# Turning the hidden chunks of five dense feed-forwards by a transposing DMA in place of TensorE

## What is computed

```python
def swiglu(h, w_gate, w_up, w_down):
    return (jax.nn.silu(h @ w_gate) * (h @ w_up)) @ w_down

x = x + swiglu(rmsnorm(x, norm), w_gate, w_up, w_down)      # second stack: 0.5 * swiglu
```

## Time and profile before

| | |
|---|---|
| time, median of 3 runs | 2066.12 us (2066.04 to 2066.29) |
| span of the profiled execution, first to last instruction | 2064.4 us |
| mean granted TensorE clock | 0.999 |
| busy: PE, DVE, ACT, POOL | 99%, 68%, 58%, 5% |
| DMA: moved, mean rate | 467.19 MB, 226 GB/s |

### The profile page before, as it was taken

The page is one execution under the profiler, slowest core; times in us unless marked ns, Lnnn a source line. Parts: engine busy times, 40 slices in busy tenths (PEclk is TensorE's granted clock), DMA queues, the critical chain, the costliest instruction groups (busy, mean ns, idle before and its releaser), DMA issues.

```text
span 2064.4 us, 27729 instructions
## 1 busy us (share of the span) xinstructions
PE 2036.4 (99%) x10169; PEld 1711.7 (83%) x10169; DVE 1411.3 (68%) x1558; ACT 1199.0 (58%) x1386; POOL 94.8 (5%) x140
## 2 busy tenths in 40 slices
PE   9999999999999999999999999999999999999999
PEld 9988888778888888887888877888888899888887
DVE  6655557688898898999554675455555579795454
ACT  4454458677777877776444565444544465875442
POOL 1010001000000000010100010000000000230000
PEclk9999999999999999999999999999999999999999
DMA  8555434389999998998555444555555455445551
GB/s 306 183 187 192 176 133 144 126 308 371 364 378 374 365 380 348 381 392 331 204 183 185 179 146 151 196 183 184 183 184 186 148 179 196 163 154 190 194 186 41
DMA packets 68273, 467.19 MB, mean 226 GB/s; under 512 B 7777, under 2 KB 8177, under 8 KB 13521
## 3 DMA queue, kind: packets, MB, share of 16 engines
q1 hardware_dynamic: 63616, 455.24, 59.5%
q10 hardware_dynamic: 3536, 8.10, 1.2%
q0 software_dynamic: 1024, 2.56, 0.5%
HBM read 461.11 MB, written 4.75 MB: 226 GB/s over the span
## 4 chain that ended last, share of the span: by engine, by line
PE 89%; DVE 5%; ACT 3%; issue 1%; DVEq 1%; ACTq 0%; POOL 0%; POOLq 0%
PE gu L2177 15%; PE gu L2179 15%; PE gu L2178 15%; PE acc L2177 10%; PE acc L2179 10%; PE acc L2178 10%; DVE wlo L1315 2%; PE acc L2273 2%; PE acc L2275 2%; PE acc L2274 2%; PE tp L2287 1%; ACT whi L715 1%; PE tp L2206 1%; PE acc L2732 1%; PE tp L2764 1%
## 5 line engine op out<-in xcount | busy, mean ns | idle before, releaser
L1315 DVE TENSOR_TENSOR wlo<-raw,whi 128x2048 fp32r<-128x2048 f32 (+2 forms) x422 | 956.4, 2270 | 351.1 <-ACT whi L715 350.4
L715 ACT ACTIVATE whi<-raw 128x2048 fp32r<-128x2048 f32 (+1 forms) x436 | 827.3, 1899 | 213.6 <-PE acc L2179 165.1
L2177 PE MATMUL gu<-whi,actA_hi 128*128 128x512 f32 x1408 | 560.0, 398 | 0.9 <-DVE wlo L1315 0.6
L2179 PE MATMUL gu<-whi,actA_lo 128*128 128x512 f32 x1408 | 549.3, 390 | 0.0
L2178 PE MATMUL gu<-wlo,actA_hi 128*128 128x512 f32 x1408 | 548.5, 390 | 0.0
L2179 PEld LDWEIGHTS gu<-whi,actA_lo 128*128 128x128 f32 x1408 | 264.7, 188 | 55.8
L2177 PEld LDWEIGHTS gu<-whi,actA_hi 128*128 128x128 f32 x1408 | 265.1, 188 | 54.5 <-issue 2.3
L2178 PEld LDWEIGHTS gu<-wlo,actA_hi 128*128 128x128 f32 x1408 | 265.4, 189 | 50.6
L2177 PE MATMUL acc<-whi,hT_hi 128*128 128x512 f32 x656 | 256.5, 391 | 0.5 <-DVE wlo L1315 0.5
L2179 PE MATMUL acc<-whi,hT_lo 128*128 128x512 f32 x656 | 255.9, 390 | 0.0
L2178 PE MATMUL acc<-wlo,hT_hi 128*128 128x512 f32 x656 | 255.7, 390 | 0.0
(11 more groups left out here) (452 smaller groups left out, 2351.5 us busy)
## 6 DMA issues: line engine op xcount, KB each, us to landing
raw<-in_slabs SPq DMA_DIRECT2D x427, 1024.0 KB, 4.9
y_rows<-big ACTq DMA_DIRECT2D x7, 512.0 KB, 5.1
raw<-in_slabs SPq DMA_DIRECT2D x4, 576.0 KB, 3.8
hT_hi<-cum_rows ACTq DMA_DIRECT2D x8, 256.0 KB, 3.9
hT_lo<-cum_rows ACTq DMA_DIRECT2D x8, 256.0 KB, 4.0
raw<-in_slabs SPq DMA_DIRECT2D x2, 768.0 KB, 4.2
raw<-in_slabs SPq DMA_DIRECT2D x2, 640.0 KB, 3.9
x<-in_x SPq DMA_DIRECT2D x2, 512.0 KB, 4.3
```

The source lines that it names most:

```text
L715: act.activation(whi[:, n0 % SPLIT, 0:w], raw[:, n0 % RAW, 0:w], ACT.Copy).then_inc(slab_hi, 1)
L1315: dve.tensor_tensor(wlo[:, n0 % SPLIT, 0:w], raw[:, n0 % RAW, 0:w], whi[:, n0 % SPLIT, 0:w].bitcast(F32), ALU.subtract).then_inc(slab_spli ...
L2177: pe.matmul(o, xh, wh, start=start, stop=False)
L2179: return pe.matmul(o, xl, wh, start=False, stop=stop)
```

## The change

In the dense feed-forwards, chunks 0 to 9 are no longer turned by PE. After the second silu, ACT waits for h_tok and copies it, seen as 16-bit integers, to two planes: the low halves of all 512 floats of a partition, then the high halves (`turned`). It waits for its own copy and issues one transposing DMA of 128x1024 16-bit elements into `h_turned`, as eight blocks of 128. At the next up_a position DVE copies the eight blocks back into floats with the halves side by side (`joined`, 1024 elements a partition), ACT makes hT_hi from that (`joined_hi`), and DVE makes hT_lo (`joined_lo`). PE's down product waits on hidden_lo. The order of the 128-column blocks in hT differs, which `hidden_cols` makes up for. Chunk 10 and the experts are turned by PE as before; a dense feed-forward counts one use of `tp` instead of 11.

```diff
@@ ffn_stage
-            stage("ffn", slabs=3 * C * experts, tp=C * experts, hi=C * experts, ...
+            turns = 1 if gates is None else C * experts
+            stage("ffn", slabs=3 * C * experts, tp=turns, hi=turns, ...
@@ views
+        h_planes = area(2560, 512).bitcast(U16).rearrange("p (w n) -> p w n", w=2)
+        h_turned = area(3072, 512).bitcast(U16).rearrange("p (b n) -> p b n", n=P)
+        hT_all = area(3584, 512)
+        hidden_halves = h_tok[:, :, :].rearrange("p t n -> p (t n)").bitcast(U16).rearrange("p (n w) -> p w n", w=2)
+        joined_halves = hT_all[:, :].bitcast(U16).rearrange("p (n w) -> p w n", w=2)
+        turned_halves = h_turned[:, :, :].rearrange("p (w b) n -> p w (b n)", w=2)
@@ ACT
+                def turned(c, i):
+                    act.wait_ge(gu_read, 2 * (f.c0 + c + 1) + 4 * i)
+                    act.activation(h_planes[:, :, :], hidden_halves, ACT.Copy).then_inc(hidden_planes, 1)
+                    act.wait_ge(hidden_planes, m0 + c + 1 + 2 * i)
+                    act.sem_inc(hidden_sent, 1)
+                    act.dma_start_transpose(h_turned[:, :, :], h_planes[:, :, :].rearrange("p w n -> p (w n)")
+                                            ).then_inc(hidden_turned, 16)
+                def joined_hi(c, i):
+                    act.wait_ge(hidden_joined, m0 + c + 1 + 2 * i)
+                    act.activation(hT[0], hT_all[:, :], ACT.Copy).then_inc(hidden_hi, 1)
...
+                        if dense and k != 3 * C - 3:
+                            turned(c, i)
+                    elif kind == "up_a" and k and dense:
+                        joined_hi(c - 1, i)
@@ DVE
+                def joined(c, i):
+                    dve.wait_ge(hidden_turned, 16 * (m0 + c + 1) + 32 * i)
+                    dve.tensor_copy(joined_halves, turned_halves).then_inc(hidden_joined, 1)
+                def joined_lo(c, i):
+                    dve.wait_ge(hidden_hi, m0 + c + 1 + 2 * i)
+                    dve.tensor_tensor(hT[1], hT_all[:, :], hT[0].bitcast(F32), ALU.subtract).then_inc(hidden_lo, 1)
...
-                        if k:
+                        if k and dense:
+                            joined(c - 1, i)
+                            joined_lo(c - 1, i)
+                        elif k:
                             t_lo(c - 1, i, ex)
@@ PE
-                        pe.wait_ge(tp_read, f.u0 + c + 1 + 2 * i + C * ex)
+                        last = c == C - 1
+                        if dense and not last:
+                            pe.wait_ge(hidden_lo, m0 + c + 1 + 2 * i)
+                        else:
+                            pe.wait_ge(tp_read, turn_at(f, c) + 1 + 2 * i + C * ex)
...
-                    if kind == "up_a" and k:
+                    if kind == "up_a" and k and not dense:
                         transposes(c - 1, i, ex)
```

More of the change, by code:

```diff
@@ L23 @@
 I32 = mybir.dt.int32
+U16 = mybir.dt.uint16
 ACT = mybir.ActivationFunctionType
@@ L147, in program @@
         out_done = sem("out_done")
+        hidden_planes = sem("hidden_planes")
+        hidden_turned = sem("hidden_turned")
+        hidden_sent = sem("hidden_sent")
+        hidden_joined = sem("hidden_joined")
+        hidden_hi = sem("hidden_hi")
+        hidden_lo = sem("hidden_lo")
         V_MIX, V_FFN, V_CONV, V_QA, V_KVA = (0, 0), (0, 16), (0, 32), (0, 56), (0, 59)
@@ L184, in ffn_stage @@
         def ffn_stage(C, scale, experts=1, gates=None):
-            stage("ffn", slabs=3 * C * experts, tp=C * experts, hi=C * experts, x=2 * experts, chunk=C * experts,
+            turns = 1 if gates is None else C * experts
+            stage("ffn", slabs=3 * C * experts, tp=turns, hi=turns, x=2 * experts, chunk=C * experts,
                   C=C, scale=scale, experts=experts, gates=gates,
@@ L497, in program, with turn_at, hidden_before, hidden_cols @@
         hT_spare = [v[:, 2 * P:4 * P] for v in (hT_hi, hT_lo)]
+        h_planes = area(2560, 512).bitcast(U16).rearrange("p (w n) -> p w n", w=2)
[4 more added lines that the diff above has]
+        turned_halves = h_turned[:, :, :].rearrange("p (w b) n -> p w (b n)", w=2)
+        def turn_at(f, c):
+            return f.u0 if f.gates is None else f.u0 + c
+        def hidden_before(f):
+            return f.fn * (f.C - 1)
+        def hidden_cols(f, j, t, at_end):
+            b = 2 * j + t if at_end or f.gates is not None else 2 * t + j
+            return slice(b * P, (b + 1) * P)
         def each_expert(e, fn):
@@ L764, in ffn @@
                 C = f.C
+                dense, m0 = f.gates is None, hidden_before(f)
                 def t_hi(c, i, ex, to=hT):
-                    act.wait_ge(tp_full, f.u0 + c + 1 + 2 * i + C * ex)
-                    act.activation(to[0], tp[:, (f.u0 + c) % 2], ACT.Copy).then_inc(tp_hi, 1)
+                    u = turn_at(f, c)
+                    act.wait_ge(tp_full, u + 1 + 2 * i + C * ex)
+                    act.activation(to[0], tp[:, u % 2], ACT.Copy).then_inc(tp_hi, 1)
+                def turned(c, i):
[8 more added lines that the diff above has]
+                    act.activation(hT[0], hT_all[:, :], ACT.Copy).then_inc(hidden_hi, 1)
                 def at(k, i, ex):
@@ L1379, in ffn @@
                 C = f.C
+                dense, m0 = f.gates is None, hidden_before(f)
                 def t_lo(c, i, ex, to=hT):
-                    dve.wait_ge(tp_hi, f.h0 + c + 1 + 2 * i + C * ex)
-                    dve.tensor_tensor(to[1], tp[:, (f.u0 + c) % 2], to[0].bitcast(F32),
+                    dve.wait_ge(tp_hi, f.h0 + (0 if dense else c) + 1 + 2 * i + C * ex)
+                    dve.tensor_tensor(to[1], tp[:, turn_at(f, c) % 2], to[0].bitcast(F32),
                                       ALU.subtract).then_inc(tp_read, 1)
+                def joined(c, i):
[4 more added lines that the diff above has]
+                    dve.tensor_tensor(hT[1], hT_all[:, :], hT[0].bitcast(F32), ALU.subtract).then_inc(hidden_lo, 1)
                 def at(k, i, ex):
@@ L2279, in ffn @@
                 C = f.C
+                dense, m0 = f.gates is None, hidden_before(f)
                 def transposes(c, i, ex):
+                    u = turn_at(f, c)
                     pe.wait_ge(gu_read, 2 * (f.c0 + c + 1) + 4 * i + 2 * C * ex)
-                    pe.wait_ge(tp_read, f.u0 + c - 1 + 2 * i + C * ex)
+                    pe.wait_ge(tp_read, u - 1 + 2 * i + C * ex)
                     for j in range(2):
                         for t in range(NT):
-                            r = pe.transpose(tp[:, (f.u0 + c) % 2, (2 * j + t) * P:(2 * j + t + 1) * P],
+                            r = pe.transpose(tp[:, u % 2, (2 * j + t) * P:(2 * j + t + 1) * P],
                                              h_tok[:, t, j * P:(j + 1) * P], ident[:, :])
@@ L2296, in at @@
                     if kind == "down":
-                        pe.wait_ge(tp_read, f.u0 + c + 1 + 2 * i + C * ex)
+                        last = c == C - 1
[3 more added lines that the diff above has]
+                            pe.wait_ge(tp_read, turn_at(f, c) + 1 + 2 * i + C * ex)
                         w = [z[:, sl].rearrange("p (j n) -> p j n", j=2) for z in (whi, wlo)]
-                        last = c == C - 1
                         h_hi, h_lo = hT_last if ends_with(f, k - 1, ex) else hT
@@ L2313, in at @@
                                 for t in range(NT):
-                                    cs = slice((2 * j + t) * P, (2 * j + t + 1) * P)
+                                    cs = hidden_cols(f, j, t, last)
                                     r = three(acc[:, 2 * t + n], h_hi[:, cs], h_lo[:, cs],
```

## The result

| | before | after |
|---|---|---|
| time, median | 2066.08 us (2065.33 to 2066.29, 4 runs) | 2043.57 us (2042.91 to 2044.56, 4 runs) |
| span of the profiled execution | 2064.4 us | 2041.2 us |
| mean granted TensorE clock | 0.999 | 0.999 |

The ratio of the times is 0.9892, 95% interval 0.9878 to 0.9906: the change makes the kernel 1.1% faster. The forecast was 2043.

What follows compares the result with a forecast made beforehand. PE alone was taken to set the pace, busy 2036.4 of 2064.4 us. Span 2064.4 - 24.0 + 1.0 (first chunks) = 2041.4, plus 1.7 from span to median, gave 2043 us; range 2040.5 to 2095.

Steps and rivals of the forecast that it cites:

- the 24.0 us: PE in the dense feed-forwards: 50 groups of four transposes removed, 0.48 us each, all of it on the path.
- the first chunks: First chunk of each of five feed-forwards: landing may be 6.0 us, margin 0.5; 1 us in all added, 0.2 each.
- The new copies: Per inner chunk: planes copy on ACT 1.08 us, join on DVE 1.24 us, both free if in time.
- The landing, L: Time of the transposing DMA from issue to semaphore, per inner chunk: taken as 5.5 us, between 1.5 and 8.7.
- The upper bound of 8.7: High end for the DMA's landing: 64 packets an engine at 0.112 us, 7.2, plus 1.5 us fixed.
- The router's load: Router weights loaded from POOL behind other loads, taken as 1024 pieces of 32 B landing in 10.9 us; kept as an end.
- my 7.2: Transfer part of the landing's high end: 64 packets on each of 16 engines at 0.112 us, 7.2 us.
- The bound on L: Longest landing that stays hidden: 8.3 us in the steady loop, 6.0 in each feed-forward's first chunk.
- The issue, X: Time the transposing DMA's issue holds ACT's queue: taken as 1.6 us, the middle between 0.35 and 2.8.
- X may be 4.4: Steady loop: the DMA issue may hold ACT 4.4 us before the slab split behind it is late for PE.
- Rival 3: Issue holds ACT over 1.9 us: at 2.8 first chunks lose 4.5, 2047; every chunk pays only over 4.4. Chance 0.07.
- Rival 2: Landing longer than the loop allows, DVE's join waits: break-even 8.6 us, at 9.0 2089, at 10.9 2184. Chance 0.22.

Runs made afterwards that it cites:

- four powers: Changed kernel with POOL waiting for the transposing DMA and making four small powers before it releases DVE's join, a later landing: 2260.48 us, ratio 1.0939.
- four quarters: Changed kernel with its one transposing DMA cut into four of two blocks each: 2217.45 us (one run beside 2066.75).

## Why the prediction was right, and where it was not

- **What bounds the kernel, and the 24.0 us.** Right. The span fell by 23.2; a chunk went from 16.79 to 16.32 us, 0.47 against 0.48, and the transposes put back took the time back to 2066.7. That 2043 was met to 0.6 us is in part luck: the 24.0 were 0.8 too many, and the 1.0 added for the first chunks was not needed.
- **The new copies.** The planes took 1.06 us against 1.08. The join took 0.75 against the bound of 1.24: the nearest row was an operation with two inputs on floats (L1572), and a copy of 1024 16-bit elements goes faster than that.
- **The landing, L.** Taken 5.5, measured 3.3 (3.0 to 5.7). The upper bound of 8.7 was far off: q10's share rose from 1.2% to 4.6%, (0.046 x 2041.2 - 0.012 x 2064.4) / 50 = 1.4 us of all engines for one DMA, 0.02 us a packet and not 0.112. The router's load was a weak witness for its 10.9 us too: all of POOL's loads in the first 40 us together have 352 packets, so it did not go as 1024 packets. The Trainium skill's 261 GB/s ("DMA: Bandwidth & Descriptors", section "Latency and other measured facts") gave an estimated 1.0 us for the transfer. The 1.4 measured are nearer to it than to my 7.2. The Trainium skill's 1309 ns for one block ("VectorE: DVE Perf Modes", section "The three transpose paths") would be an estimated 10.5 us for eight in turn. The whole landed in 3.3, so that price is not paid eight times.
- **The bound on L.** "L may be 8.3 us" in the loop and 6.0 in the first chunk. Right in kind: the feedback through hT_hi, split and h_tok is real (four powers). In size 8.8 and 6.4, since the join is 0.5 us shorter.
- **The issue, X.** Taken 1.6, measured 1.25 to 1.87. But **"X may be 4.4" is the step that failed.** I bounded it by the slab behind the issue alone, and put only the landing into the loop. The join stands behind two of DVE's splits, and these behind ACT's and the issue; so the issue has a branch of its own, 13.99 + X, and may be 2.3 us. Rival 3 thus lay much nearer than its price says: at the 2.8 us that I named as its upper end it would have cost 0.5 us in each inner chunk, not only 0.9 in five. The forecast held because X was 1.25. My 1.6 was only the middle between 0.35 and 2.8, so that X lay under 2.3 was luck and not reasoning.
- **The first chunks.** 1 us in all was allowed for them; they cost nothing. Their margin is 0.25 to 0.48 us in the trace, against 0.5 reckoned, but the two sides are not those of the sum: the split is later (the issue took 1.59 to 1.87) and the join shorter. In other kernels with one issue it took up to 3.1 us there, so this margin is thin.
- **Rival 2, slower.** Its mechanism is real, with the price as told; its condition was far off, 8.6 us where the landing took 3.3. For an L of 12.89 us the prediction's formula gives 2283 us; the kernel whose join started that late took 2260, since the bounds are 8.8 and 6.4 and not 8.3 and 6.0.

## What to carry to other kernels

When work leaves the bounding engine for a path over others, compare two lengths: the deadline of each result, and one whole turn of the loop on the engines that now carry it, with every instruction in their order, the issuing of a DMA among them. In the loop the second was the tighter here: 1.1 us of margin where the reckoned deadlines left 3 us or more. At the beginning, before the loop is full, it was a deadline: 0.25 us. A wait that is placed behind other work of its engine puts that work into the loop; moving it ahead took it out, and cost nothing while the landing was early.

## What was not expected of the hardware

- A transposing DMA holds the queue that issues it for 1.25 us, whether it has 8 blocks or 2 (1.18); the plain one of the same planes holds it 0.47. It moves 256 KB from SBUF to SBUF in 3.3 us to the semaphore, 0.9 us more than the plain one.
- Two in a row are slower to issue than one: the second took 1.34 us at the least and up to 3.7.
- A 2.3 us wait of PE was followed by 3 us at a granted clock of 0.50. In the kernel with four powers, where PE waits in every chunk, the mean over the run is 0.96, with four quarters 0.98, and 0.999 in the kernels before and after.
